# Stick-breaking attention with queries on partitions, in a two-layer decoder trunk

## What is computed

```python
def _stick_breaking(q, k, v):
    ...
        z = jnp.einsum('bhqd,bhkd->bhqk', qb, k).astype(jnp.float32) * scale
        qpos = c0 + jnp.arange(Q_BLOCK, dtype=jnp.int32)
        mask = kpos[None, :] < qpos[:, None]
        log1m = jnp.where(mask, jax.nn.log_sigmoid(-z), 0.0)
        between = lax.cumsum(log1m, axis=3, reverse=True) - log1m
        a = jnp.where(mask, jnp.exp(jax.nn.log_sigmoid(z) + between), 0.0)
        return jnp.einsum('bhqk,bhkd->bhqd', a.astype(v.dtype), v)
...
x = x + merged @ w_out[l]
x = x + (jax.nn.silu(hn @ w_ffn_gate[l]) * (hn @ w_ffn_up[l])) @ w_ffn_down[l]
```

## Time and profile before

| | |
|---|---|
| median of 3 runs | 827.85 us (827.54 to 828.66) |
| profiled execution | 828.2 us, span 826.4 us |
| PE busy | 821.6 us (99%) |
| DVE busy | 559.7 us (68%) |
| ACT busy | 477.8 us (58%) |
| POOL busy | 293.7 us (36%) |
| granted PE clock | 1.00 of full |
| DMA | 167.76 MB, 203 GB/s on average |

### The profile page before, as it was taken

One profiled execution on the slowest core, in us unless ns is written; L12 is line 12 of the kernel. 1 busy time (PEld: TensorE's weight loads), 2 busy tenths in 40 slices (PEclk: granted clock), 3 DMA queues, 4 the chain that ended last, 5 costly groups with the idle time before them and its releaser, 6 DMA issues.

```text
span 826.4 us, 11044 instructions
## 1 busy us (share of the span) xinstructions
PE 821.6 (99%) x4050; PEld 673.7 (82%) x4050; DVE 559.7 (68%) x821; ACT 477.8 (58%) x715; POOL 293.7 (36%) x297
## 2 busy tenths in 40 slices
PE   9999999999999999999999999999999999999998
PEld 5888888888888888888888888888788888888886
DVE  5576889868865666655454688898697666666542
ACT  6886655785465554543457775567844645454441
POOL 0078784404303432320000889653061044323100
PEclk9999999999999999999999999999999999999999
DMA  9745877684558777785565556878745687877652
GB/s 332 271 138 178 222 230 219 182 247 131 203 178 229 199 230 212 223 221 183 167 203 195 162 192 192 224 222 210 223 153 178 206 214 218 230 223 212 215 184 71
DMA packets 119637, 167.76 MB, mean 203 GB/s; under 512 B 56608, under 2 KB 59040, under 8 KB 119328
## 3 DMA queue, kind: packets, MB, share of 16 engines
q1 hardware_dynamic: 119296, 166.79, 66.9%
q10 hardware_dynamic: 288, 0.27, 0.1%
HBM read 153.40 MB, written 1.05 MB: 187 GB/s over the span
## 4 chain that ended last, share of the span: by engine, by line
PE 98%; DMA 1%; issue 0%; SPq 0%; ACT 0%; DVE 0%
PE acc L732 91%; PE att L812 1%; PE att L895 1%; PE att L779 1%; PE att L886 1%; DMA w_raw<-in_w_in 1%; PE att L804 1%; PE acc L812 1%; PE att L853 0%; PE att L869 0%; PE att L908 0%; PE att L972 0%; PE att L963 0%; PE att L854 0%; PE att L839 0%
## 5 line engine op out<-in xcount | busy, mean ns | idle before, releaser
L1234 DVE TENSOR_TENSOR w_lo<-w_raw,w_hi 128x1024 fp32r<-128x1024 f32 (+1 forms) x276 | 365.4, 1337 | 147.1 <-ACT w_hi L996 144.6
L732 PE MATMUL acc<-w_hi,xt 128*128 128x512 f32 (+1 forms) x1728 | 432.3, 392 | 0.5 <-ACT xt L1019 0.3
L996 ACT ACTIVATE w_hi<-w_raw 128x1024 fp32r<-128x1024 f32 (+1 forms) x275 | 286.1, 1051 | 168.7 <-PE acc L732 159.1
L732 PEld LDWEIGHTS acc<-w_hi,xt 128*128 128x128 f32 x1728 | 319.0, 188 | 66.3 <-issue 1.3
L732 PE MATMUL acc<-w_lo,xt 128*128 128x512 f32 (+1 forms) x864 | 229.9, 388 | 0.0
L732 PEld LDWEIGHTS acc<-w_lo,xt 128*128 128x128 f32 x864 | 162.0, 188 | 32.9
L1485 POOL TENSOR_SCALAR small<-small 128x2 f32<-128x2 f32 (+4 forms) x14 | 10.4, 745 | 209.2 <-ACT sq_dump L1096 132.4
L1617 POOL COPY hid_t<-hid_halves_t 128x512 uint16<-128x512 uint16 x44 | 37.7, 885 | 94.3 <-DMA hid_halves_t<-hid_halves 80.0
L1608 POOL COPY hid_halves<-hid 128x512 uint16<-128x512 uint16 x44 | 45.6, 1064 | 65.2 <-DVE hid L1311 65.2
L1625 POOL TENSOR_TENSOR merged<-merged,prod 128x1024 f32<-128x1024 f32 x10 | 32.5, 3250 | 61.2 <-DVE prod L1283 60.3
L732 PE MATMUL acc<-w_hi,ht_hi 128*128 128x512 f32 x176 | 47.7, 390 | 0.0
(11 more groups left out here) (175 smaller groups left out, 723.5 us busy)
## 6 DMA issues: line engine op xcount, KB each, us to landing
w_raw<-in_w_ffn SPq DMA_DIRECT2D x88, 512.0 KB, 4.2
w_raw<-in_w_gate SPq DMA_DIRECT2D x64, 512.0 KB, 3.9
w_raw<-in_w_ffn_down SPq DMA_DIRECT2D x44, 512.0 KB, 4.0
w_raw<-in_w_in SPq DMA_DIRECT2D x39, 512.0 KB, 4.7
w_raw<-in_w_branch SPq DMA_DIRECT2D x16, 512.0 KB, 4.1
w_raw<-in_w_out SPq DMA_DIRECT2D x16, 512.0 KB, 3.3
bg<-in_b_gate SPq DMA_DIRECT2D x8, 512.0 KB, 5.4
w_raw<-in_w_in SPq DMA_DIRECT2D x8, 396.0 KB, 3.4
```

Of the source, the lines that this page charges most:

```text
L732: return pe.matmul(acc[bank0 + t][:, 0:N], x_part[:, k0 + k, t * P:(t + 1) * P], w_part[:, k, 0:N], start=first, stop=last)
L996: act.activation(w_hi[:, n % WR, :, 0:N], w_raw[:, n % RAW, :, 0:N], copy).then_inc(s_hi, 1)
L1234: dve.tensor_tensor(w_lo[:, n % WR, :, 0:N], w_raw[:, n % RAW, :, 0:N], w_hi[:, n % WR, :, 0:N].bitcast(F32), ALU.subtract).then_inc(s_lo, 1)
```

## The change

Mixer A gets its queries on partitions. Scores of all four heads are made at chunk 9 (`sm` A, the second pair in idle accumulators), and DVE adds the mask while it reads them (`strict_add`). ACT makes Abs and Exp at 10 and Ln at 11, now over 4 maps of 384 columns at once; DVE makes the softplus at 12 (`ssum`), sums over later keys by four `tensor_tensor_scan` with reversed columns at 13 and 14 (`restart` holds a zero where a block ends), and subtracts at 15 (`ssub`); ACT takes exp at 17. The weights then have keys on columns, so they are transposed as C's and D's are: `pdeal` at 18, DMA transposes issued by SyncE at its chunks 26 and 27, `pjoin` at 23 and 24, `pv` at 27. The mask product, the triangular products and the constants for them go. Output pair 0 moves from 22 to 28, B's first `pv` from 27 to 29, `prep` C from 18 to 19. The compressed keys `kcs` are padded with zeros to 128 rows, and `kct` is a matmul with the identity's first 16 columns. The constants in one load grow from 960 to 1216 columns, and the separate masks' load goes.

```diff
 WARM_UP = 12
 RAW, WR, LEAD = 4, 4, 2
 STATS_0 = 3
-TURNS = [("C", 0), ("C", 1), ("D", 0), ("D", 1), ("D", 2), ("D", 3)]
-TURN_P = (43, 47, 52, 53, 55, 56)
+TURNS = [("A", 0), ("A", 1), ("C", 0), ("C", 1), ("D", 0), ("D", 1), ("D", 2), ("D", 3)]
+TURN_P = (26, 27, 43, 47, 52, 53, 55, 56)
 TURN_AT = {33: "C", 40: "D"} | {CHUNKS.index(("ffn", j, 3)) + 9: j for j in range(N_FFN)}


...

 PLAN = {
     "stats": 1, "stats_f": 3, "lambda": 14, "x": (0, 0, 1, 2), "f": (-2, -1, 2, 3), "m": (-1, -1, 2, 3),
-    "sig": (49, 53, 57, 57), "o": (22, 45, 48, 58), "subln": 40, "prep": (13, 18, 25), "ngate": 25, "Aq": 6,
-    "Ak": 7, "Az": (9, 14), "Asp": (9, 14), "Acum": (13, 17), "Apv": (21, 21), "Bq": 19, "Bk": 20,
-    "Bsm": (21, 21, 27, 27), "Bp": (21, 24, 27, 29), "Bpt": (24, 27, 29, 32), "Bpv": (27, 29, 33, 35), "Bo": 36,
+    "sig": (49, 53, 57, 57), "o": (28, 45, 48, 58), "subln": 40, "prep": (13, 19, 25), "ngate": 25, "Aq": 6,
+    "Ak": 7, "Asm": (9, 9), "sabs": 10, "sln": 11, "ssum": 12, "sscan": (13, 14), "ssub": 15,
+    "sexp": 17, "Apdeal": (18, 18), "Apjoin": (23, 24), "Apv": (27, 27), "Bq": 19, "Bk": 20,
+    "Bsm": (21, 21, 27, 27), "Bp": (21, 24, 27, 29), "Bpt": (24, 27, 29, 32), "Bpv": (29, 29, 33, 35), "Bo": 36,
     "Cdeal": 24, "Cjoin": 30, "Csm": (35, 35), "Cp": (35, 38), "Cpdeal": (36, 39), "Cpjoin": (41, 45), "Cpv": (46, 46), "Dc": 27,
     "cbuild": 29, "ck": 31, "cks": 31, "cv": 31, "kcprep": 32, "kct": 37, "cr": 35, "cs": 39, "cp": 39,
     "cpt": 43, "cpv": 51, "Ddeal": 31, "Djoin": 35, "Dsm": (42, 42, 46, 46), "Dp": (42, 42, 46, 47),
...
         big = top[0]
         proj = place("proj", [P, NT, IN_COLS], F32)
-        p_halves, p_halves_t = ([place(f"{name}{i}", [P, 2, 2, 384], U16, at=big + t * (4 * IN_COLS + 16) + 12 * i * MIX)
-                                 for i in range(2)] for t, name in enumerate(("p_halves", "p_halves_t")))
         zg = place("zg", [P, NT, 4, D_MODEL], F32)
         zg_at = big + NT * IN_COLS * 4
         zg_at += (-zg_at) % 32
         end_big = top[0]
+        za = place("za", [P, 4, 384], F32, at=zg_at + 4 * D_MODEL)
+        turn_at = {"p_halves": (zg_at + 16 * D_MODEL, big), "p_halves_t": (zg_at + 22 * D_MODEL, big + 4 * IN_COLS + 16)}
+        p_halves, p_halves_t = ([place(f"{name}{2 * j + i}", [P, 2, 2, 384], U16, at=at + 12 * i * MIX)
+                                 for j, at in enumerate(starts) for i in range(2)] for name, starts in turn_at.items())
...

-        mask32 = eb[:, 0, 0:P]
         causal_add = cst[:, C_MK:C_MK + 2 * P]
-        ident, negtri, negone = cst[:, C_ID:C_ID + P], cst[:, C_TRI:C_TRI + P], cst[:, C_ONE:C_ONE + P]
-        ident16, mask_a = (cst16[:, i * P:(i + 1) * P] for i in range(2))
+        strict_add = cst[:, C_MK:C_MK + 3 * P].rearrange("p (b k) -> p b k", k=P)[:, 0:3:2, :]
...
-                                  mask_a.unsqueeze(1).to_broadcast([P, 2, P]), start=True, stop=False, skip_group_check=True)
                 if mixer == "B":
                     score_matmuls(l, sum(todo, []))
                 else:
                     for maps in todo:
-                        score_matmuls(l, maps, swap=kind == "z")
-
-            def cumulate(l, step):
-
-                pe.wait_ge(dve_misc.sem, dve_misc.at(l, ("sp", step[1])))
-                for h in range(2):
-                    for i in range(2):
-                        b, part = S0 + h, sp_parts[:, h, i, :]
-                        pe.matmul(att[:, b, 0:384], tri_r[:, 0, :], part, start=False, stop=False, skip_group_check=True)
-                        mm = pe.matmul(att[:, b, P:2 * P], tri_r[:, 1, :], part[:, 256:384], start=False, stop=i == 1,
-                                       skip_group_check=True)
-                mm.then_inc(att_done.now(step), 1)
+                        score_matmuls(l, maps)

...
                             mm = pe.matmul(att[i * HD:(i + 1) * HD, OB, n * SEQ + s * P:(n + 1) * SEQ], proj[:, s, v:v + HD],
-                                           ptb[:, 2 * (m % 2) + i, 2 * s * P:(2 + s) * P],
+                                           (za if mixer == "A" else ptb)[:, 2 * (m % 2) + i, 2 * s * P:(2 + s) * P],
                                            start=mixer != "D" and s == 0, stop=s == NT - 1, skip_group_check=True)
...
                             pe.wait_ge(pool_done.sem, pool_done.at(l, ("kcprep", None)))
-                            pe.transpose(att[:, TP, 0:16], kcs[:, :, :], ident[0:16, 0:16]
-                                         ).then_inc(att_done.now(step), 1)
+                            pe.matmul(att[:, TP, 0:16], kcs[:, :, :].rearrange("p m d -> p (m d)"), ident[:, 0:16],
+                                      start=True, stop=True).then_inc(att_done.now(step), 1)
...
-                        ins = act.activation(zt1, att[:, S0:S0 + 2, 0:384] if f == ACT.Abs else zt1, f, **kw)
-                        ins.then_inc(s_zc, 1)
-                        softplus_chain[0] += 1
-                        if f != ACT.Ln:
-                            act.wait_ge(s_zc, softplus_chain[0])
-
-                elif kind == "cum":
-                    act.wait_ge(att_done.sem, att_done.at(l, step))
-                    pb = pt_free(l, step)
-                    act.activation(ptb[:, pb:pb + 2, :], att[:, S0:S0 + 2, 0:384], ACT.Exp
-                                   ).then_inc(read_act.now(step), 1)
-                elif kind == "sm":
+                elif kind == "sabs":
+                    act.wait_ge(read_dve.sem, read_dve.at(l, ("sm", ("A", 1))))
+                    act.activation(za[:, :, :], eb[:, :, :], ACT.Abs).then_inc(s_zc, 1)
+                    act.wait_ge(s_zc, 2 * l + 1)
+                    act.activation(za[:, :, :], za[:, :, :], ACT.Exp, scale=-1.0).then_inc(s_zc, 1)
+                elif kind == "sln":
+                    act.wait_ge(s_zc, 2 * l + 2)
+                    act.activation(za[:, :, :], za[:, :, :], ACT.Ln, bias=1.0).then_inc(act_misc.now(step), 1)
+                elif kind == "sexp":
+                    act.wait_ge(dve_misc.sem, dve_misc.at(l, ("ssub", None)))
+                    act.activation(eb[:, :, :], eb[:, :, :], ACT.Exp).then_inc(act_misc.now(step), 1)
+                elif kind == "sm" and a[0] != "A":
                     exps(l, step)
                 elif kind == "pt":
                     act.wait_ge(att_done.sem, att_done.at(l, step))
...
                     act.wait_ge(s_pturn[k % 2], p_turned(l, a))
-                    pb = pt_free(l, step)
+                    if a[0] == "A":
+                        dst = za[:, 2 * a[1]:2 * a[1] + 2, :]
+                    else:
+                        pb = pt_free(l, step)
+                        dst = ptb[:, pb:pb + 2, :]
                     for i in range(2):
-                        ins = act.activation(ptb[:, pb + i, :].bitcast(U16).rearrange("p (c s) -> p s c", s=2),
-                                             p_halves_t[k % 2][:, i, :, :], copy)
+                        ins = act.activation(dst[:, i, :].bitcast(U16).rearrange("p (c s) -> p s c", s=2),
...
+                        act.wait_ge(s_init, 5)
                     for m in range(2):
-                        ins = act.activation(kcs[:, m, :], att[0:16, TP, 0:HD], copy)
+                        ins = act.activation(kcs[0:16, m, :], att[0:16, TP, 0:HD], copy)
                     ins.then_inc(read_act.now(step), 1)
                 elif kind == "kcprep":
...
             dve.memset(vblk[:, :, :], 0.0).then_inc(s_init, 1)
             dve.memset(cpb[:, :, :, :], 0.0).then_inc(s_init, 1)
             dve.memset(kct[:, :, :], 0.0).then_inc(s_init, 1)
-            dve.wait_ge(s_init, 4)
+            dve.memset(kcs[:, :, :], 0.0).then_inc(s_init, 1)
+            dve.wait_ge(s_init, 5)
...
+                        e, bank = e_of(step)[0][i], score_bank(l, step, i)
+                        dve.tensor_tensor(eb[:, e, 0:P], bank[:, 0:P], strict_add[:, 1, :], ALU.add)
+                        ins = dve.tensor_tensor(eb[:, e, P:384].rearrange("p (b k) -> p b k", k=P),
+                                                bank[:, P:384].rearrange("p (b k) -> p b k", k=P), strict_add, ALU.add)
+                    ins.then_inc(read_dve.now(step), 1)
+                elif kind == "ssum":
+                    dve.wait_ge(act_misc.sem, act_misc.at(l, ("sln", None)))
+                    settled(dve.scalar_tensor_tensor(out=za[:, :, :], in0=eb[:, :, :], scalar=0.0, in1=za[:, :, :],
                                                      op0=ALU.max, op1=ALU.add))
-                    hi, lo = (sp_parts[:, :, i, :] for i in range(2))
-                    settled(dve.tensor_copy(hi, zt2))
-                    dve.tensor_tensor(lo, zt2, hi.bitcast(F32), ALU.subtract).then_inc(dve_misc.now(step), 1)
+                elif kind == "sscan":
+
+                    for h in (2 * a, 2 * a + 1):
+                        ins = dve.tensor_tensor_scan(out=za[:, h, ::-1], data0=restart[:, ::-1], data1=za[:, h, ::-1],
```

(21 more changed lines are left out.)

130 lines of the change are left out of this document (49 added, 81 removed).

## The result

The changed kernel takes 854.42 us (median of 4 runs, 852.16 to 854.77) against 827.98 us for the kernel before (827.54 to 828.66): a ratio of 1.0313, with an interval of 1.0298 to 1.0327. It is 26.4 us slower. The direction and the three places were forecast, but the size was given as 12.65 us, and the time lies 8.4 us above the range. The profiled execution took 854.4 us with a span of 852.6. Two executions far outside, one of the kernel before (1174 us) and one of the kernel with B's preparation first (4398 us), are left out of every ratio.

What follows compares the result with a forecast made beforehand. PE, busy 821.6 of 826.4 us, was taken to set the time. 827.85 + 4.05 (first wait) + 2 x (0.8 + 3.7) - 0.4 (keys) gave 840.5 us; range 825 to 846.

Steps and rivals of the forecast that it cites:

- the three places: Chunks 19, 27 and 29, where PE would wait on POOL, on ACT, and on the copy of output pair 0.
- What bounds the kernel, what PE loses: PE's program sets the time; it loses 3.0 us of work a layer, 6.1 in two, reaching chunk 19 at 62.7.
- First wait: Chunk 19: B's query transposes wait 4.2 us for POOL's `prep` B; against before, 1.35 plus 2.7 us lost, 4.05.
- The walk to POOL's start: Steps of ACT and DVE ahead of `prep` B: POOL starts at 48.4 instead of 46.55, 2.9 us late in layer two.
- rival (d): Same three waits, with DVE's added two-input instructions delaying POOL in `prep` B: 3 us more a layer, 846.5 us; chance 0.08.
- the low halves that were to be 0.4 to 1 us early: DVE's splits of chunks 16 to 18, put off by the scans: ready 0.4 to 1 us before PE wants them.
- Second wait: Chunk 27: PE waits 0.8 us for ACT, which has four added joins of A's weights; bounds 0 to 2.
- Third wait: Chunk 29: B's value products wait 3.7 us for the copy of A's output pair 0; bounds 1.5 to 5.
- What is hidden: DMA transposes at chunks 25 to 27, later `prep` C and D, and the larger constants load: costed at nothing.
- The forecast sum: First wait 4.05, twice second and third (0.8 + 3.7), less 0.4 for the keys: 12.65 us.
- What would show it: Signs: PE's waits at 19, 27 and 29, POOL's first power at 49.5, scan duration, two or three table loads by 19.
- POOL's chain far from 18.4: Sign against the forecast: POOL's run of instructions for `prep` B, ahead of chunk 19, not lasting about 18.4 us.

Runs made afterwards that it cites:

- the kernel with B's preparation first: The changed kernel with mixer A's Ln and later steps moved to chunks 13 to 18, behind B's squares and reduction: 853.36 us, ratio 1.0309.
- the fill kernel: The changed kernel with unread 512-column products on PE, five before B's query transposes and three before B's first value products: 843.88 us, ratio 1.0191.
- the kernel with late joins and filler: The changed kernel with A's joins at 28, value products at 30 and 33, output copy at 31, and five unread products before B's query transposes: 839.39 us.
- the kernel with all steps spread out: The changed kernel with A's Ln to exp at 13 to 18, B's query transposes at 21, joins at 29, value products at 31 and 33: 845.63 us.
- the one with B's queries at 20: The changed kernel with A's Ln and later steps at 13 to 18, A's joins at 28, B's transposes at 20 and 21: 839.53 us.
- the one with both repairs: The changed kernel with B's transposes at 21 and 22, A's joins at 28, value products at 30 and 33, output copy at 31: 846.71 us.
- the kernel with B's queries at 21: The changed kernel with B's transposes at 21 and 22, C's preparation at 21, A's DVE steps at 12 to 17, joins unmoved: 850.57 us.
- the late order: The changed kernel with A's joins at 28, value products at 30, output copy at 31, B's first value products at 33: 842.53 us, ratio 1.0177.

## Why the prediction was wrong in size

Point by point, in its own order.

*What bounds the kernel, what PE loses.* Right to 0.3 us. PE reaches chunk 19 at 63.88, of which 0.88 is its wait for `w_lo`: 63.0, forecast 62.7.

*First wait.* The walk to POOL's start held to 0.1 us: 48.48 for 48.4, and in the second layer 2.9 us late for 2.9 (472.49 less the 14.18 by which that layer begins later, against 455.40). ACT's instructions of 1536 columns took 1.49 each for 1.5. Two things failed here. The chain was 20.0 us long, not 18.4; I had given 1.4 to 3 us either way and then taken the row of before "since DVE is as full there after the change". That reason was the wrong step: DVE was as full, but with more instructions that read two operands from SBUF, and these hold POOL. My rival (d), at 0.08, had this mechanism and priced it at 3 us a layer; it was 1.6. So PE was held by 3.3 and 4.4 us against before, in place of 1.35 and 2.7 (the second from 492.66 less 474.06, its start in the timeline of before, less 14.18). And the low halves that were to be 0.4 to 1 us early came 0.9 us late; as forecast, this only changed where PE waited.

*Second wait.* 1.27 us in the first layer and 0.4 in the second, for 0.8: in the bounds.

*Third wait.* 2.74 us in each layer for 3.7, in its bounds 1.5 to 5. Counted from chunk 27, PE came 1.2 us later than walked (9.7 us for 8.5), with small waits of 0.3 and 0.2 us on its way, and DVE's low half was ready 0.2 later.

*What is hidden.* Held for PE: no wait of PE for the moved transposes is listed; landing took 3.7 to 6.2 us. `pdeal` ended at 72.5, not at 71.1, and SyncE waited for it once, 0.3 us.

*The missing term.* The forecast sum, 12.65 us, prices a wait at its length. With the measured terms it would be 7.7 (first wait) + 1.7 + 5.5 - 0.3 = 14.6, which is in the range. The work at the low clock behind the four long waits, compared with the fill kernel, is 8.5 us more, together 23.1 of 26.4. The step that failed is therefore a term set at zero without a row: after a stall, PE was assumed to go on at the 1.00 at which the whole of before ran. Before had no wait above 1.2 us, so its trace could not show the fall; that was a reason to bound it at up to double the work behind a wait, not to leave it out.

Of the remaining 3.3 us, listed waits explain 1.3: `w_hi` at 84.94 (0.4), `kcvt` (0.6) and `small` (0.3). The waits for `w_lo` stand before chunk 19 and are part of the first term: what PE waits for a low half at 62 it need not wait at 68. The most of the rest is probably that a stall costs more than its listed length. Without one, a step's row begins 0.16 us or more before the modelled end of the row ahead of it; behind a stall it can't, and nine stalls give some 1.5 us (an estimate from the timelines). Where low halves come only just in time, the four products of one take 1.20 us (58.79) instead of 1.07 and begin some 0.3 us late without a wait being listed. The 2.6 us that the listed waits leave open in the kernel with late joins and filler are likely of the same kind, with ten stalls. These last readings are argued, not tested.

*What would show it.* The named waits came, POOL's power began at 49.68 (49.5), the scan pair took 1.8 us (1.6, bounds 1.0 to 2.0), and by chunk 19 there were two table loads in the first layer and three in the second. The granted clock was not among the signs. "POOL's chain far from 18.4" was named as what would make it wrong.

## What to carry to other kernels

Where PE is 99% busy, ask of each added wait how long PE will stand still: a few tenths cost little more than themselves, while the four waits of 2.7 and 4.8 us cost 1.6 to 3.2 us each on top, because the products behind them ran at the 1.2 GHz level. When work moves from PE to DVE, count what DVE takes from POOL too, above all if a chain of POOL already ends within a microsecond of its user. Moving steps in a full schedule moves the collision: four orders here made one wait smaller and another one larger.

## What the runs showed of the hardware that I had not expected

The granted clock does not follow the length of a wait alone. Over all kernels here that have such waits, all 16 of 3.0 to 4.8 us were followed or accompanied by 0.50, and 9 of the 10 of 2.7 to 2.8 us. Of the 12 of 1.65 to 2.25 us, 3 were: 1.72 us in the kernel with all steps spread out, 1.93 in the one with B's queries at 20, and 2.23 in the one with both repairs. The one exception near 2.7 is 2.76 us in the kernel with B's queries at 21, which left the clock full:

```profile
104.76 1.52 PE L857 MATMUL att<-proj,ptb 128*128 128x64 f32 x12 [2.76 <-DVE ot_lo L1207]
106.00:108.00 2.00, 2.00 (x13) 1.74 (x13) 1.99 (x4) 1.34 (x2) 1.86 (x4) 1.00 0.45 169
```

Nor does it always fall while PE stands still. By the windows view it fell in the kernel after near 66.3, in the middle of the first wait; in the second layer's third wait, 2.74 us up to 529.29, it was still 1.00 at the end and fell near 530.5, when PE had worked for 1.2 us.

Scatter may go with it: the executions of the late order lie over 4.0 us and those of the changed kernel over 2.6, while the two with fillers lie over 0.7 and 0.6. Against it stands the kernel with all steps spread out, whose clock falls three times and whose four executions lie within 0.1. This was not tested.

DVE and POOL slow each other by whole instructions: a 64-column rotation of POOL takes 0.29 us alone and 1.27 or 1.80 beside two-input instructions, a split of DVE 1.22 elsewhere and 2.76 beside POOL's multiplications. The trace agrees with what "SBUF — State Buffer" of the Trainium skill (section SBUF: two separate sides) says, that the loser of the shared ports waits for the whole of the other's instruction.

A scan took 0.94 us for 384 columns, 2.5 ns a column, where the softplus sum over 1536 columns took 1.75 us, 1.1 ns a column; the start of an instruction is a larger share of the shorter one. The trace agrees with the half throughput that the Trainium skill gives it ("DVE: opcode table, instruction layouts, handler registers and perf-mode slots", section 6, feedback).
